# One channel tile of a 31-tap convolution: products on ScalarE, added up by accumulating DMAs

## The chip, the cores and the metric

The kernel runs on one core of one Trainium2 chip. The metric is the device time of one execution in microseconds (us), lower is better. The engines are named as in the profile: PE is TensorE (matrix products; PEld is its weight load), DVE is VectorE, ACT is ScalarE, POOL is GpSimd, SP is SyncE. An engine works through its own instruction list in order; engines wait for one another through semaphores.

## The reference

The reference runs two transformer blocks of two layers each on 512 tokens of width 1024. The change is in the second block, first layer, where the 512 tokens and 256 context tokens (768 in all) go through `conv_mixers`:

```python
def conv_mixers(h, w_in, conv_a, conv_b, conv_b_bias, ln_g, ln_b, w_out):
    p = h @ w_in
    g_b, g_c, u_a, v_b, gate_b = jnp.split(
        p, [A_WIDTH, 2 * A_WIDTH, 3 * A_WIDTH, 3 * A_WIDTH + B_WIDTH], axis=-1)
    y_a = g_b * dwconv(g_c * u_a, conv_a)
    u = v_b * jax.nn.sigmoid(gate_b)
    u = dwconv(u, conv_b) + conv_b_bias
    y_b = jax.nn.silu(layernorm(u, ln_g, ln_b))
    return jnp.concatenate([y_a, y_b], axis=-1) @ w_out
```

`conv_b` is a depthwise convolution with 31 taps over the tokens: each of its 512 channels is a sum of 31 shifted copies of its own row, each times one weight. The 512 channels are four tiles of 128. Everything is float32.

## The kernel before

Channels lie on the 128 partitions and tokens along the free dimension. A matrix product runs in "blocks": a block is one tile of 128 output channels for all tokens. Its 128x1024 weights come from HBM into `w_raw` (SP, L468), are rounded into `w_hi` by ScalarE (L675) and the remainder is written to `w_lo` by VectorE (L1201, function `split`); then TensorE multiplies high by high, high by low, and low by high (L1851, L1852, L1853). Weights have four slots and sums have four places in PSUM, so an engine can be some three blocks ahead of another. `w_hi` of a block is written three blocks ahead of its use.

The input product of the mixer has 20 blocks, in three stages:

- `mix_c`, 8 blocks: `v_b` and `gate_b`, tile by tile. After the second block of tile q, ScalarE takes the sigmoid (L791) and VectorE writes the product into the padded row `padded(q)` (L1393): `u_pad[:, q, :]` for tiles 0 to 2, `wk[:, 1, :]` for tile 3 (`wk` is a view of `work`).
- `mix_a`, 8 blocks: `g_c` and `u_a`. ScalarE copies one (L775), VectorE multiplies (L1409) and does the three-tap convolution into `conv_a` (L1411, L1335, L1338).
- `mix_b`, 4 blocks: `g_b`. VectorE multiplies by `conv_a` (L1422), ScalarE writes the high part `a_hi` (L782), VectorE the low part `a_lo` (L1313).

Then come `layernorm` and the output product `w_out`. Of `w_out` TensorE does the half that needs only `y_a` (k 0 to 3 of its first two blocks) at the head of its `layernorm`; then it waits until all four tiles of `conv_out` are there (semaphore `conv`), and sums them over the channels (L1885). The centring (L1432), squares (L800), their sums (L1890), the root on GpSimd (L523), its spreading (L1860) and the scaling (L1443) follow one after another, and the rest of `w_out` after them.

The 31-tap convolution is done wholly by VectorE, in `conv_taps(first, last)`. It numbers 124 taps (4 tiles x 31), keeps the running sum of a tile in `wk[:, 3, :]` over 783 columns (512 tokens, 15 of padding, 256 context tokens), and writes the last tap into `conv_out` (L1376, two instructions). Tap 0 of a tile is L1370, taps 1 to 29 are L1372. The taps are dealt out by hand over the blocks: 7 after each block of `mix_c` but the first, 6 after each of `mix_a`, 7 after each of `mix_b`. Each stands in VectorE's list behind the `split` of a coming block and the evacuation of the present one, so the taps fix how late VectorE comes to both. GpSimd has nothing to do from the norm's root before `mix_c` to the root of the layernorm.

Of the kernel before, what the change touches and what calls it, by code (L numbers as in the profile page):

```python
# [7 lines left out]
F32 = mybir.dt.float32  # L8
# [3 lines left out]
ALU = mybir.AluOpType  # L12
# [3 lines left out]
P = 128  # L16
D = 1024
KT_D = D // P
SEQ = 512
# [8 lines left out]
HALO = 15  # L28
U_COLS = HALO + SEQ + HALO + CTX + HALO


# [135 lines left out]
def program(nc, dram, out):  # L167
    stages = make_plan()
    stack = ExitStack()
    with stack:  # L170
# [3 lines left out]
        def sem(name):  # L174
            return stack.enter_context(nc.semaphore(name))
# [40 lines left out]
        def layout(*items):  # L216
# [9 lines left out]


        _, conv_a, u_pad, _, conv_out = layout(
            ("mix_gap", [P, 12 * D], F32), ("conv_a", [P, 4, ALL], F32), ("u_pad", [P, 3, 832], F32),
            ("mix_gap2", [P, 6 * D - 3 * 832], F32), ("conv_out", [P, 4, ALL], F32))  # L230

# [34 lines left out]
        def ps_of(st, s, a=0, b=ALL):  # L266

            if st["toks"] == SEQ:
# [29 lines left out]
        s_val = sem("gate_times_value")  # L298
        s_out = sem("out_stored")
        s_const = sem("constants_ready")  # L300
        s_constb = sem("bf16_ready")
# [17 lines left out]
        s_swt = {t: {k: sem(f"sw{t}_{k}") for k in sw_names if t == "a" or k not in only_a}  # L319
                 for t in ("a", "b")}  # L320

        LOADS_IN = 4
# [195 lines left out]
        def _(pool):  # L518
# [61 lines left out]
            for st in stages:  # L580
                if st["kind"] == "norm":
                    root(0, st["toks"] // P, s_ms, st["rms0"] + 1, s_pw)
                elif st["kind"] == "layernorm":
                    root(0, 6, s_ln["ms"], 1, s_ln["pw"])
# [35 lines left out]
        def _(act):  # L620
# [127 lines left out]
            def evac_cffn(st):  # L748
# [19 lines left out]
                return f  # L768

            def evac_mix_a(st):  # L770
                def f(b, s, i):
                    if s % 2 == 0:
                        act.wait_ge(s_mm, b + (st["block0"] + 1))
                        act.wait_ge(s_ev, b + (st["lin0"] + 4))
                        act.activation(wk[:, 0, 0:ALL], ps_lin(s), ACT.Copy).then_inc(s_gate, 1)  # L775
                        act.drain()
                return f

# [7 lines left out]
            def evac_mix_c(st):  # L786
                def f(b, s, i):
                    if s % 2 == 1:
                        act.wait_ge(s_mm, b + (st["block0"] + 1))
                        act.wait_ge(s_ev, b + (st["lin0"] + 3))  # L790
                        act.activation(wk[:, 0, 0:ALL], ps_lin(s), ACT.Sigmoid).then_inc(s_gate, 1)  # L791
                        act.drain()
                return f

# [298 lines left out]
        def _(dve):  # L1093
# [267 lines left out]
            def conv_taps(first, last):  # L1361

                n = SEQ + HALO + CTX
                acc = wk[:, 3, 0:n]
                for tap in range(first, last):
                    q, j = tap // 31, tap % 31
                    u = padded(q)
                    w = vcol("conv_b", tap)
                    if j == 0:
# [11 lines left out]
            def evac_mix_c(st):  # L1381
# [4 lines left out]
                def f(b, s, i):  # L1386
# [9 lines left out]
                    if b:  # L1396
                        conv_taps(7 * (b - 1), 7 * b)
                return f

            def evac_mix_a(st):  # L1400
                base = VEC["conv_a"][0]

                def f(b, s, i):
                    if s % 2 == 1:
# [9 lines left out]
                                   vec[:, bass.ds(q + (base + 8), 1)], ALL)  # L1414
                    conv_taps(49 + 6 * b, 55 + 6 * b)
                return f

            def evac_mix_b(st):
                def f(b, s, i):
                    t = wk[:, 2 * (s % 2), 0:ALL]  # L1420
                    dve.wait_ge(s_mm, b + (st["block0"] + 1))
                    dve.tensor_tensor(t, ps_lin(s), conv_a[:, b, :], ALU.mult).then_inc(s_ev, 1)  # L1422
                    dve.drain()
                    low_part(b, t, ALL, b + (st["tile0"] + 1))
                    dve.drain()
                    conv_taps(97 + 7 * b, min(104 + 7 * b, 124))
                return f
# [956 lines left out]
```

## Time and profile before

| | us |
|---|---|
| median of 3 runs | 3028.74 |
| lowest, highest | 3027.15, 3029.84 |
| the profiled execution | 3028.09 |
| its span, first to last instruction | 3026.3 |
| TensorE busy | 2786.0 (92%) |
| VectorE busy | 1836.8 (61%) |
| ScalarE busy | 1080.0 (36%) |
| GpSimd busy | 118.8 (4%) |

The shares are means over a program of many stages. The stretch in question lasts from about 1404.9 us (TensorE's first matmul of `mix_c`) to about 1655 us of the span; its rows stand further down. The clock column of a row, PEclk, is the share of TensorE's full clock of 2.4 GHz that was granted; 0.50 is 1.2 GHz. "us" on a row of a timeline is the time from the start of the first to the end of the last of the instructions it merges.

### The profile page before, as it was taken

What the parts mean: (1) busy time and instruction counts of PE and PEld (TensorE: products, weight loads), DVE (VectorE), ACT (ScalarE), POOL (GpSimd) and SP (SyncE); (2) the same over time, 40 slices, a digit from 0 to 9 for tenths busy, and PEclk for the clock granted to TensorE, in tenths of its full rate; (3) what the DMA queues carried; (4) which work ended last, traced back from release to release, by engine and by line L of the source; (5) the groups of instructions that cost most, each with busy time, mean ns of one, the idle gap of its engine ahead of it and who ended that gap; (6) DMA issues with size and microseconds to landing.
All of it is one profiled execution on the core that took longest, in us unless ns stands there. A gap on an engine that the chain in (4) does not pass through costs nothing.

```text
span 3026.3 us, 41051 instructions
## 1 busy us (share of the span) xinstructions
PE 2786.0 (92%) x14220; PEld 2339.0 (77%) x14220; DVE 1836.8 (61%) x2910; ACT 1080.0 (36%) x1778; POOL 118.8 (4%) x148
## 2 busy tenths in 40 slices
PE   7999899997787999998986899999997899899998
PEld 6777788886676788887875788888886787688886
DVE  6766567676565577667996554353455455564645
ACT  5444332223565322223112232232223566352432
POOL 4111000000110000000000000000000000000000
PEclk8999999998898999998997999999998999999999
DMA  3111254452001355542110122122111000232321
GB/s 110 63 56 43 98 187 167 171 182 72 29 29 36 112 180 174 175 155 68 56 49 30 48 70 70 56 65 68 54 58 42 15 29 8 70 97 91 97 89 65
DMA packets 69314, 252.07 MB, mean 83 GB/s; under 512 B 7840, under 2 KB 10144, under 8 KB 66592
## 3 DMA queue, kind: packets, MB, share of 16 engines
q1 hardware_dynamic: 69152, 249.99, 24.5%
q8 instruction: 92, 1.51, 0.2%
q14 instruction: 70, 0.57, 0.1%
HBM read 247.87 MB, written 2.10 MB: 83 GB/s over the span
## 4 chain that ended last, share of the span: by engine, by line
PE 61%; DVE 16%; issue 15%; ACT 4%; DVEq 2%; POOLq 0%; ACTq 0%; POOL 0%; DMA 0%; SPq 0%
PE psum L1852 16%; PE psum L1851 16%; PE psum L1853 16%; DVE work L1372 4%; PE psum L2233 2%; DVE w_lo L1201 1%; ACT work L991 1%; PE psum L1991 1%; ACT sw_pt L1003 1%; PE psum L1969 1%; PE psum L1971 1%; PE psum L1970 1%; DVE neg_max L1740 1%; DVE tok_ms L1489 1%; DVE w_lo L1566 1%
## 5 line engine op out<-in xcount | busy, mean ns | idle before, releaser
L1851 PE MATMUL psum<-hx_hi,w_hi 128*128 128x512 f32 x1568 | 623.9, 398 | 28.9 <-DVE w_lo L1201 13.5
L1852 PE MATMUL psum<-hx_lo,w_hi 128*128 128x512 f32 x1568 | 625.1, 399 | 0.0
L1853 PE MATMUL psum<-hx_hi,w_lo 128*128 128x512 f32 x1568 | 623.7, 398 | 0.0
L675 ACT ACTIVATE w_hi<-w_raw 128x1024 fp32r<-128x1024 f32 (+1 forms) x328 | 344.6, 1051 | 527.2 <-PE psum L1853 231.4
L1201 DVE TENSOR_TENSOR w_lo<-w_raw,w_hi 128x1024 fp32r<-128x1024 f32 (+1 forms) x328 | 397.7, 1212 | 192.6 <-ACT w_hi L675 174.0
L1851 PEld LDWEIGHTS psum<-hx_hi,w_hi 128*128 128x128 f32 x1568 | 297.1, 189 | 79.1 <-issue 16.7
L1853 PEld LDWEIGHTS psum<-hx_hi,w_lo 128*128 128x128 f32 x1568 | 297.1, 189 | 69.9
L1852 PEld LDWEIGHTS psum<-hx_lo,w_hi 128*128 128x128 f32 x1568 | 298.0, 190 | 48.4
L1851 PE MATMUL psum<-a_hi,w_hi 128*128 128x512 f32 (+1 forms) x656 | 234.1, 357 | 18.1 <-DVE a_lo L1313 10.0
L1852 PE MATMUL psum<-a_lo,w_hi 128*128 128x512 f32 (+1 forms) x656 | 234.8, 358 | 0.0
L1853 PE MATMUL psum<-a_hi,w_lo 128*128 128x512 f32 (+1 forms) x656 | 233.9, 357 | 0.0
L1851 PE MATMUL psum<-o_hi,w_hi 128*128 128x512 f32 x544 | 217.8, 400 | 5.6 <-DVE o_lo L1778 3.9
L1852 PE MATMUL psum<-o_lo,w_hi 128*128 128x512 f32 x544 | 216.8, 398 | 0.0
L1853 PE MATMUL psum<-o_hi,w_lo 128*128 128x512 f32 x544 | 216.7, 398 | 0.0
L1335 DVE SCALAR_TENSOR_TENSOR work<-psum,vec,work 128x511 f32<-128x511 f32 (+1 forms) x132 | 83.2, 658 | 164.3 <-ACT work L758 156.3
L523 POOL TENSOR_TENSOR tok_r<-tok_ms,half 128x4 f32<-128x4 f32 (+1 forms) x70 | 71.8, 1025 | 2502.2 <-DVE tok_ms L1115 1949.6
L1277 DVE SCALAR_TENSOR_TENSOR X<-psum,mods,X 128x512 f32<-128x512 f32 x96 | 60.6, 658 | 178.6 <-PE psum L1853 177.1
L1851 PEld LDWEIGHTS psum<-a_hi,w_hi 128*128 128x128 f32 x656 | 125.2, 191 | 38.5 <-DVE a_lo L1313 10.5
L758 ACT ACTIVATE work<-psum,vec 128x768 f32<-128x768 f32 (+1 forms) x88 | 70.0, 795 | 223.5 <-PE psum L1853 215.8
L1852 PE MATMUL psum<-hc_lo,w_hi 128*128 128x256 f32 x512 | 144.8, 283 | 0.0
L1851 PE MATMUL psum<-hc_hi,w_hi 128*128 128x256 f32 x512 | 144.8, 283 | 0.0
L1853 PE MATMUL psum<-hc_hi,w_lo 128*128 128x256 f32 x512 | 144.5, 282 | 0.0
(289 smaller groups left out, 4914.2 us busy)
## 6 DMA issues: line engine op xcount, KB each, us to landing
mod_w<-in_w_mod SPq DMA_DIRECT2D x96, 512.0 KB, 3.6
w_raw<-in_fup SPq DMA_DIRECT2D x88, 512.0 KB, 4.5
w_raw<-in_cup SPq DMA_DIRECT2D x88, 512.0 KB, 3.5
w_raw<-in_fdown SPq DMA_DIRECT2D x32, 512.0 KB, 4.6
w_raw<-in_cdown SPq DMA_DIRECT2D x32, 512.0 KB, 3.5
w_raw<-in_da_qkv SPq DMA_DIRECT2D x6, 1536.0 KB, 6.5
w_raw<-in_fdown SPq DMA_DIRECT2D x16, 384.0 KB, 3.1
w_raw<-in_cdown SPq DMA_DIRECT2D x16, 384.0 KB, 3.0
```

Of the source, the lines that this page charges most:

```text
L523: pool.tensor_tensor(tok_r[:, a:b], tok_ms[:, a:b], half[:, a:b], ALU.pow).then_inc(done, 1)
L675: r = act.activation(w_hi[:, off:off + n], w_raw[:, raw:raw + n], ACT.Copy)
L758: act.activation(wk[:, s, 0:toks], ps_of(st, s, 0, toks), ACT.Copy, scale=vec[:, bass.ds(b + col, 1)]).then_inc(s_ctap, 1)
L991: r = act.activation(work[:, e:e + (w1 - w0)], psum[:, w0:w1], ACT.Exp, bias=neg_max[:, col:col + 1], scale=root, accum_out=row_sum[:, col ...
L1201: r = dve.tensor_tensor(w_lo[:, off:off + n], w_raw[:, raw:raw + n], w_hi[:, off:off + n].bitcast(F32), ALU.subtract)
L1277: r = dve.scalar_tensor_tensor(X[:, b, a:e], ps_of(st, s, a, e), mods[:, l, c, bass.ds(b + o, 1)], X[:, b, a:e], ALU.mult, ALU.add)
L1335: dve.scalar_tensor_tensor(dst[:, a + 1:e], src(a, e - 1), prev, dst[:, a + 1:e], ALU.mult, ALU.add)
L1372: dve.scalar_tensor_tensor(acc, u[:, j:j + n], w, acc, ALU.mult, ALU.add)
L1851: pe.matmul(dst, wh, xh, start=first, stop=False)
L1852: pe.matmul(dst, wh, xl, start=False, stop=False)
L1853: return pe.matmul(dst, wl, xh, start=False, stop=last)
L2233: r = pe.matmul(pb[:, 5, 0:256], v_cols(tiles[k], g, p % 2), sw_pt[:, n % 2, 256 * i:256 * i + 256], start=p % 2 == 0 and k == 0, stop=p % ...
```

## The change

Tile 1 of the convolution is taken from VectorE. The running sums of that tile are two, in the two halves of `sw_vb`, a buffer that attention uses in other stages.

- **ScalarE** forms the 31 products: `tap_products` writes weight times shifted row, 783 columns, one instruction a tap (L800 and L803 of the new kernel). Taps 0 and 1 go straight into the two sums, with the bias in tap 0; taps 2 to 30 go into four buffers `tap_prod` in turn. Three products stand at the end of each block's work on ScalarE, from the fifth block of `mix_c` (after a wait for tile 1 of `u_pad`) to the sixth of `mix_a`, and the last one at its seventh. From tap 6 on each waits until the DMA that read its buffer last, that of tap j-4, has landed.
- **GpSimd** issues 29 DMAs, `tap_prod` into `sw_vb` with addition, even taps into sum 0, odd taps into sum 1. A DMA waits for its product and for the DMA before it on the same sum.
- **VectorE** keeps tiles 0, 2 and 3: 93 taps, dealt out 6 a block in `mix_c`, 4 and 5 in turn in `mix_a`, 4 a block in `mix_b` (3 in the last). In the first block of `mix_b`, behind the multiplication of the evacuation and before `low_part`, it waits for both sums and adds them into `conv_out[:, 1]`.

```diff
+                elif st["kind"] == "mix_a":
+                    for j in range(2, TAPS):
+                        pool.wait_ge(s_tapp, j + 1)
+                        if j >= 4:
+                            pool.wait_ge(s_taps[j % 2], taps_added(j - 2))
+                        pool.dma_start(tap_sum(j % 2), tap_prod[:, j % TAP_BUFS, 0:TAP_COLS], accum_op=ALU.add)\
+                            .then_inc(s_taps[j % 2], 16)
...
+            def tap_products(first, last):
+
+                u = padded(SUM_TILE)
+                for j in range(first, min(last, TAPS)):
+                    w = vcol("conv_b", TAPS * SUM_TILE + j)
+                    if j >= 2 + TAP_BUFS:
+                        act.wait_ge(s_taps[j % 2], taps_added(j - TAP_BUFS))
+                    dst = tap_sum(j) if j < 2 else tap_prod[:, j % TAP_BUFS, 0:TAP_COLS]
+                    if j == 0:
+                        act.activation(dst, u[:, j:j + TAP_COLS], ACT.Identity, scale=w, bias=vcol("conv_b_bias", SUM_TILE))\
+                           .then_inc(s_tapp, 1)
+                    else:
+                        act.activation(dst, u[:, j:j + TAP_COLS], ACT.Copy, scale=w).then_inc(s_tapp, 1)
+                    act.drain()
+
             def evac_mix_a(st):
...
+                    tap_products(12 + 3 * b, 15 + 3 * b)
...
+                    if b == 2 * SUM_TILE + 2:
+                        act.wait_ge(s_ev, st["lin0"] + 2 * SUM_TILE + 6)
+                    if b >= 2 * SUM_TILE + 2:
+                        first = 3 * (b - 2 * SUM_TILE - 2)
+                        tap_products(first, first + 3)
...
-                        conv_taps(7 * (b - 1), 7 * b)
+                        conv_taps(6 * (b - 1), 6 * b)
...
-                    conv_taps(49 + 6 * b, 55 + 6 * b)
+                    conv_taps(42 + 9 * b // 2, 42 + 9 * (b + 1) // 2)
...
+                    if b == 0:
+                        for c in range(2):
+                            dve.wait_ge(s_taps[c], taps_added(TAPS - 1 - c))
+                        for a, e, c in segs(ALL):
+                            o = HALO * c
+                            r = dve.tensor_tensor(conv_out[:, SUM_TILE, a:e], tap_sum(0)[:, o + a:o + e],
+                                                  tap_sum(1)[:, o + a:o + e], ALU.add)
+                        r.then_inc(s_ln["conv"], 1)
+                        dve.drain()
                     low_part(b, t, ALL, b + (st["tile0"] + 1))
                     dve.drain()
-                    conv_taps(97 + 7 * b, min(104 + 7 * b, 124))
+                    conv_taps(78 + 4 * b, min(82 + 4 * b, 93))
```

ScalarE's list where the sixth and seventh blocks of `mix_c` are evacuated, before: the weights of a coming block, the sigmoid of the present one, the weights of the next two.

```order
780 L675 ACTIVATE w_hi<-w_raw 128x1024 [waits block_multiplied,raw_loaded3]
781 L675 ACTIVATE w_hi<-w_raw 128x1024 [waits block_multiplied,raw_loaded0]
782 L791 ACTIVATE work<-psum 128x768 [waits psum_evacuated,block_multiplied]
783 L675 ACTIVATE w_hi<-w_raw 128x1024 [waits block_multiplied,raw_loaded1]
784 L675 ACTIVATE w_hi<-w_raw 128x1024 [waits block_multiplied,raw_loaded2]
```

The same place after the change (L696 is what L675 was, L828 what L791 was):

```order
784 L696 ACTIVATE w_hi<-w_raw 128x1024 [waits block_multiplied,raw_loaded0]
785 L828 ACTIVATE work<-psum 128x768 [waits psum_evacuated,block_multiplied]
786 L803 ACTIVATE tap_prod<-u_pad,vec 128x783 x3
787 L696 ACTIVATE w_hi<-w_raw 128x1024 [waits block_multiplied,raw_loaded1]
788 L803 ACTIVATE tap_prod<-u_pad,vec 128x783 [waits tap_added_to_sum0]
789 L803 ACTIVATE tap_prod<-u_pad,vec 128x783 [waits tap_added_to_sum1]
790 L803 ACTIVATE tap_prod<-u_pad,vec 128x783 [waits tap_added_to_sum0]
791 L696 ACTIVATE w_hi<-w_raw 128x1024 [waits block_multiplied,raw_loaded2]
```

The weights of every coming block now stand behind products, and those behind waits for the DMAs of four taps before.

VectorE's list at the last block of `mix_a` and the first of `mix_b`, before: six taps, the split, the end of tile 2 and the start of tile 3 are near; at the first block of `mix_b` only the multiplication and the low part stand ahead of the taps.

```order
1384 L1372 SCALAR_TENSOR_TENSOR work<-u_pad,vec,work 128x783
1385 L1376 SCALAR_TENSOR_TENSOR conv_out<-u_pad,vec,work 128x512
1386 L1376 SCALAR_TENSOR_TENSOR conv_out<-u_pad,vec,work 128x256
1387 L1370 TENSOR_SCALAR work<-work,vec 128x783
1388 L1372 SCALAR_TENSOR_TENSOR work<-work,vec 128x783 x3
1389 L1201 TENSOR_TENSOR w_lo<-w_raw,w_hi 128x1024 [waits w_hi_ready]
1390 L1422 TENSOR_TENSOR work<-psum,conv_a 128x768 [waits block_multiplied]
1391 L1313 TENSOR_TENSOR a_lo<-work,a_hi 128x768 [waits a_hi_ready]
1392 L1372 SCALAR_TENSOR_TENSOR work<-work,vec 128x783 x7
```

The same place after (L1243 is the split, L1465 the multiplication, L1355 the low part, L1415 a tap):

```order
1384 L1415 SCALAR_TENSOR_TENSOR work<-work,vec 128x783 x5
1385 L1243 TENSOR_TENSOR w_lo<-w_raw,w_hi 128x1024 [waits w_hi_ready]
1386 L1465 TENSOR_TENSOR work<-psum,conv_a 128x768 [waits block_multiplied]
1387 L1472 TENSOR_TENSOR conv_out<-sw_vb 128x512 [waits tap_added_to_sum1,tap_added_to_sum0]
1388 L1472 TENSOR_TENSOR conv_out<-sw_vb 128x256
1389 L1355 TENSOR_TENSOR a_lo<-work,a_hi 128x768 [waits a_hi_ready]
1390 L1415 SCALAR_TENSOR_TENSOR work<-work,vec 128x783 x4
```

The joining of the two sums has come between the multiplication and the low part, and fewer taps follow.

## Rows read from the trace of the kernel before

**Rows 1.** The chain that ended last, 1400 to 1680 us: shares by line.

```profile
by line: DVE work L1372 42.8%; DVE w_lo L1201 8.8%; issue 4.1%; PE psum L1851 3.9%; PE psum L1852 3.7%; PE psum L1853 3.7%; PE psum L1890 3.2%; PE psum L1885 2.5%; DVE hx_lo L1470 2.1%; DVE work L1479 2.1%; DVEq L1379 1.9%; DVE a_lo L1313 1
```

**Rows 2.** Waits, 1425.3 to 1622 us: who waited for whom, us, times, longest.

```profile
ACT work L775 <- DVE work L1409: 39.2, 3, 16.8
PE psum L1851 <- DVE w_lo L1201: 21.7, 4, 11.7
PE psum L1851 <- DVE a_lo L1313: 6.0, 1, 6.0
DVE a_lo L1313 <- ACT a_hi L782: 3.6, 4, 0.9
```

**Rows 3.** Timeline of VectorE: start, us, instructions merged.

```profile
1429.90 6.58 DVE L1372 SCALAR_TENSOR_TENSOR work<-u_pad,vec,work 128x783 f32<-128x783 f32 x6
1436.55 1.23 DVE L1201 TENSOR_TENSOR w_lo<-w_raw,w_hi 128x1024 fp32r<-128x1024 f32 x1
...
1469.68 1.15 DVE L1376 SCALAR_TENSOR_TENSOR conv_out<-u_pad,vec,work 128x512 f32<-128x512 f32 x2
1470.92 0.69 DVE L1370 TENSOR_SCALAR work<-u_pad,vec 128x783 f32<-128x783 f32 x1
1471.69 3.25 DVE L1372 SCALAR_TENSOR_TENSOR work<-u_pad,vec,work 128x783 f32<-128x783 f32 x3
...
1554.83 1.23 DVE L1201 TENSOR_TENSOR w_lo<-w_raw,w_hi 128x1024 fp32r<-128x1024 f32 x1
...
1564.21 0.96 DVE L1409 TENSOR_TENSOR work<-psum,work 128x768 f32<-128x768 f32 x1 [0.19 <-issue]
...
1612.32 0.96 DVE L1422 TENSOR_TENSOR work<-psum,conv_a 128x768 f32<-128x768 f32 x1
...
1620.83 1.15 DVE L1376 SCALAR_TENSOR_TENSOR conv_out<-work,vec 128x512 f32<-128x512 f32 x2
```

**Rows 4.** Timeline of VectorE: the product of `mix_c`, a 512- and a 256-column tensor_tensor.

```profile
1447.01 1.02 DVE L1393 TENSOR_TENSOR u_pad<-psum,work 128x512 f32<-128x512 f32 x2 [0.16 <-issue]
```

**Rows 5.** Timeline of ScalarE; in brackets the idle time before and its releaser.

```profile
1433.11 1.06 ACT L675 ACTIVATE w_hi<-w_raw 128x1024 fp32r<-128x1024 f32 x1 [4.97 <-PE psum L1853]
1441.45 0.82 ACT L791 ACTIVATE work<-psum 128x768 f32<-128x768 f32 x1 [7.28 <-PE psum L1853]
...
1458.25 0.81 ACT L791 ACTIVATE work<-psum 128x768 f32<-128x768 f32 x1 [7.28 <-PE psum L1853]
...
1475.05 0.81 ACT L791 ACTIVATE work<-psum 128x768 f32<-128x768 f32 x1 [7.28 <-PE psum L1853]
...
1647.66 0.93 ACT L804 ACTIVATE work<-work,vec 128x768 f32<-128x768 f32 x1
1648.67 0.84 ACT L807 ACTIVATE a_hi<-work 128x768 fp32r<-128x768 f32 x1
```

**Rows 6.** Busy time by stretch: us, PE, PEld, DVE, ACT, POOL, PEclk, DMA share, GB/s.

```profile
1424.60:1542.20 117.60, 115.77 (x661) 100.86 (x660) 108.97 (x115) 20.90 (x22) 0.00 (x0) 1.00 0.19 59
1592.30:1600.40 8.10, 0.01 (x1) 0.04 (x1) 7.56 (x8) 0.00 (x0) 0.00 (x0) 0.68 0.00 0
1622.00:1629.20 7.20, 7.12 (x16) 3.53 (x16) 0.01 (x1) 0.00 (x0) 0.00 (x0) 0.76 0.00 0
1629.20:1658.00 28.80, 21.27 (x101) 19.60 (x102) 13.80 (x15) 12.84 (x14) 1.32 (x1) 0.64 0.01 1
```

**Rows 7.** DMA issues of the whole program: KB each, median us from issue to landing.

```profile
w_raw<-in_cdown SPq DMA_DIRECT2D x16, 384.0 KB, 3.0
...
w_raw<-in_in_a SPq DMA_DIRECT2D x8, 512.0 KB, 3.5
...
w_raw<-in_g_q SPq DMA_DIRECT2D x4, 1024.0 KB, 4.9
...
second_raw<-in_da_qkv SPq DMA_DIRECT2D x2, 768.0 KB, 9.2
```

**Rows 8.** Groups of GpSimd over the whole program: count, busy us, mean ns, idle before.

```profile
L523 POOL TENSOR_TENSOR tok_r<-tok_ms,half 128x4 f32<-128x4 f32 x66 | 66.5, 1007 | 1233.7 <-DVE tok_ms L1115 923.4 <-DVE tok_ms L1491 310.3
```

More of the change, by code:

```diff
@@ L29 @@
 U_COLS = HALO + SEQ + HALO + CTX + HALO
+TAPS = 31
+TAP_COLS = SEQ + HALO + CTX
+SUM_TILE = 1
+TAP_BUFS = 4
 VEC_COLS = [("attn_norm0", 8), ("attn_norm1", 8), ("ffn_norm0", 8), ("ffn_norm1", 8), ("kv_norm", 8),
@@ L225, in program @@
             ("a_hi", [P, 8, ALL], F32R), ("a_lo", [P, 8, ALL], F32R))
-        _, conv_a, u_pad, _, conv_out = layout(
+        _, conv_a, u_pad, tap_prod, conv_out = layout(
             ("mix_gap", [P, 12 * D], F32), ("conv_a", [P, 4, ALL], F32), ("u_pad", [P, 3, 832], F32),
-            ("mix_gap2", [P, 6 * D - 3 * 832], F32), ("conv_out", [P, 4, ALL], F32))
+            ("tap_prod", [P, TAP_BUFS, 912], F32), ("conv_out", [P, 4, ALL], F32))
         _, mod_c, mod_w3, mod_out, _, mod_w = layout(
@@ L299, in program @@
         s_out = sem("out_stored")
+        s_tapp = sem("tap_product_ready")
+        s_taps = [sem(f"tap_added_to_sum{c}") for c in range(2)]
         s_const = sem("constants_ready")
@@ L320, in program, with tap_sum, taps_added @@
                  for t in ("a", "b")}
+        def tap_sum(c):
+            return sw_vb[:, c, 0:TAP_COLS]
+        def taps_added(j):
+            return 16 * (j // 2)
         LOADS_IN = 4
@@ L1361, in conv_taps @@
             def conv_taps(first, last):
-                n = SEQ + HALO + CTX
+                n = TAP_COLS
                 acc = wk[:, 3, 0:n]
+                tiles = [q for q in range(4) if q != SUM_TILE]
                 for tap in range(first, last):
-                    q, j = tap // 31, tap % 31
+                    q, j = tiles[tap // TAPS], tap % TAPS
                     u = padded(q)
-                    w = vcol("conv_b", tap)
+                    w = vcol("conv_b", TAPS * q + j)
                     if j == 0:
```

## The prediction

> **What bounds the kernel now.** TensorE is 92% busy over the program, so the first question is whether VectorE's time is worth anything in this stretch. The chain that ended last answers it: from 1400 to 1680 us it runs over the taps (L1372, 42.8%) and the splits (L1201), TensorE's blocks having under 4% a line [rows 1]. The waits say the same: TensorE stood 21.7 us for `w_lo` and 6.0 us for `a_lo`, both VectorE's, and ScalarE 39.2 us for one VectorE line; VectorE waited for others only 3.6 us, 0.9 in each block of `mix_b` for ScalarE's `a_hi` [rows 2]. The timeline of VectorE then gives places and prices [rows 3], that of ScalarE the ends of TensorE's blocks: it is released at 1433.11, 1441.45, 1458.25 and 1475.05, which is 8.4 us a block at full clock [rows 5, 6]. VectorE ends its taps at 1621.98, and TensorE starts the layernorm's sums 0.05 us later. I number the 20 blocks from 0.
>
> **What leaves VectorE.** Six plain taps take 1429.90 to 1436.55, 1.108 each; a first tap 0.77 (1470.92 to 1471.69), a last tap with its two halves 1.24 (1469.68 to 1470.92) [rows 3]. Tile 1 is 29 x 1.108 + 0.77 + 1.24 = 34.1 us.
>
> **What it gets.** The joining is two tensor_tensors of 512 and 256 columns. The nearest pair is L1393, 1.02, with 0.16 of issue ahead and 0.08 behind: 1.26 [rows 4]. It stands where VectorE idles 0.9 for `a_hi` [rows 2], so it adds 0.3. Net: -33.8 us, if every VectorE instruction can start when the one before it ends, and the sums are there.
>
> **Is TensorE the next bound?** The taps are dealt out anew, so I subtract at each place what stands ahead of it less. Block 15: before at 1564.21 [rows 3] behind 91 taps, now 73: 18 plain ones less, 1544.3. TensorE ends block 7 at 1475.05 and block 15 at 1475.05 + 8 x 8.4 = 1542.2 [rows 5]. VectorE is later by 2.1, and by 2 in all of `mix_a` (it takes 16.8 us for two blocks, as TensorE does). Block 19: before at 1612.32, less 26 plain taps, a first and a last, plus 0.3: 1581.8, against 1575.9 for TensorE. The half of `w_out` behind it ends 2.9 + 2.1 us after 1581.8, at 1586.8; the taps end at 1621.98 - 33.8 = 1588.2. So VectorE stays the bound, with TensorE 2 us behind it: this saving cannot be much enlarged, but it is not cut either.
>
> **ScalarE.** A product of 783 columns is not in the trace; 768 columns take 0.84 and 0.93, 1.01 from start to start with the drain [rows 5]. With 0.98 it is 31 x 0.98 = 30 us, 2.9 in a block. ScalarE idles 7.3 ahead of each sigmoid [rows 5], and `w_hi` is made three blocks ahead, so by itself this costs nothing. Without that cover it would be 2.9 us a block.
>
> **The adding DMAs.** Here the prediction is decided, and no row shows one. Call L the time from one DMA of a sum to the next of the same sum. From the table of issues: 512 KB land in 3.5 us, 1024 KB in 4.9 [rows 7], which is 2.1 + 1.4 per 512 KB. One tap is 128 x 783 x 4 bytes, 391 KB. An addition must read product and sum, so I count 783 KB: 4.2. GpSimd has to issue it; its small instructions take 1.0 [rows 8]. The other sum's DMA and the weights share the engines: 0.3. I take L = 5.5. Ends: 3.0 (384 KB, a plain load) and 9.2 (768 KB beside many others) [rows 7]; the first is a copy without addition, the last was in a queue at the program's start, so I stay by the sum between.
>
> What L costs: product 3 is written after the sigmoid of block 5 (1458.25 + 0.81), at 1460.1, and DMA 3 is issued then. DMA 25 is the twelfth of its sum, 3, 5 to 25, and lands at 1460.2 + 12 L at the earliest once the chain is saturated. Product 29 waits for it, and behind product 29 in ScalarE's list is `w_hi` of block 17, together 2.2 us. VectorE comes to the split of block 17 at 1554.83 [rows 3] less 16 taps, 1537.1. So nothing is lost up to 12 L = 74.7, **L = 6.2**; beyond that each us of L delays the end by 12 us, and the gain is gone at L = 6.2 + 33.8 / 12 = 9.0. With L = 5.5 the last DMA lands before 1545 while VectorE comes to the joining at about 1557, so the joining waits for nothing. Below 6.2, L doesn't matter.
>
> **The clock behind it.** The layernorm's first sums take 7.1 us at a mean granted clock of 0.76; they follow a stretch in which TensorE stood 8.1 us in one piece, its clock falling to 0.68 and less [rows 6]. Now TensorE works without a gap of over 2 us from block 0 on, as it did from 1424.6 to 1542.2 at 1.00. Those sums at full clock are 7.2 x 0.76 = 5.5: -1.7. At worst the clock is at its half there, 11 us, +3.8; at best the following stretch at 0.64 gets some too, some 4 us more [rows 6]. I take -1.7.
>
> **Sum.** The profiled execution took 3028.1, 0.6 under the median of 3028.7. 3028.1 - 33.8 - 1.7 = 2992.6, a gain of 1.2%.
>
> **Rivals.**
>
> *GpSimd is held up by VectorE.* In this kernel GpSimd has worked only in pauses of VectorE's dependents, so no row shows it issuing into a VectorE that is 93% busy (108.97 of 117.6 us, rows 6). If a DMA has to let two VectorE instructions of about 1.03 pass, L is about 7.5, the end comes 12 x 1.3 = 15.6 later, TensorE's pauses come back and with them the low clock: 3028.1 - 33.8 + 15.6 = 3010. For it: the splits and taps leave only 0.08 between them. Against: an instruction list of one engine that must wait for another's has no row here at all. The Trainium skill (SBUF — State Buffer, section "Who interferes with whom") says that VectorE instructions with two SBUF inputs contend with GpSimd's reads, and only its two-port modes lock out descriptor writing; by that rule the taps would not hold the DMAs and this rival would fall. No run here shows it yet.
>
> *The two sums' DMAs do not overlap* (the slower side). They go over one queue and the same 16 engines. If the second starts only when the first has landed, L is twice one DMA, 2 x 5.2 = 10.4: 12 x 4.2 = 50 us, against 33.8 gained, 3044. It decides from 4.5 us a DMA. The same comes out if the addition itself runs at half the rate of a load. For it: nothing here shows two DMAs of one queue at work on the same tile. Against: the 16 engines are busy to 0.19 in this stretch [rows 6], so there is room, and each sum has its own semaphore.
>
> *L near 9*, the far row: 3028.1 - 33.8 + 12 x 2.8 = 3028, no change.
>
> *VectorE's taps get longer beside the DMAs.* 93 taps at +0.1 would be 9 us; no row for or against. I count it to the first rival.
>
> **How the numbers follow.** The forecast (L up to 6.2) gets 0.60: the sum of rows is 5.5 with 0.7 to spare. GpSimd held up 0.14, L near 9 0.07, not overlapping 0.19. The likeliest case alone spans 2988 (clock) to 2998. The range takes in the first rival and L up to 9.5, 3028.1 - 33.8 + 39.6 = 3034: 2988 to 3034, leaving out the slower rival's 0.19. A measurement of this kernel can tell some 0.2%, 6 us. Faster by more: 0.60 + 0.14 = 0.74. Within: 0.07. Slower: 0.19.
>
> **What would show it.** Taps ending near 1588 instead of 1622, 93 of them at 1.03; no wait of VectorE for a sum in the first block of `mix_b`; no wait of TensorE for `w_lo` over 2 us before block 20; a clock of 1.00 up to the layernorm's sums, and these in 5.5 us. Starts of adding DMAs on one sum under 6.2 apart. Wrong would be: ScalarE idle before products with the DMA as releaser, VectorE idle before the split with `w_hi` as releaser, or taps longer than 1.03.

## The result, and the profile after

| | before | after |
|---|---|---|
| median of 4 runs, us | 3029.09 | 3000.85 |
| lowest to highest | 3027.15 to 3029.84 | 2996.45 to 3004.93 |
| the profiled execution | 3028.09 | 2996.45 |
| its span | 3026.3 | 2994.6 |

The ratio of the times is 0.9907, 95% interval 0.9892 to 0.9922: faster by 0.9%. The forecast was 2992.6 in a range of 2988 to 3034, and its direction and range held; the gain is 28.2 us by the medians and 31.6 by the profiled executions, where 35.5 were forecast. The runs of after lie further apart than those of before; eight further runs of the same kernel (below) lie between 2994.8 and 2999.7, and the median of all twelve is 2997.4.

To compare two executions I measure from the start of VectorE's `tok_ms` in the norm ahead of `mix_c` (1396.5 in before's span) and not from the start of the span, because the code ahead of it, the same in both, took 1395.7 to 1401.7 us in the profiles of this study. "Stretch" below is the time from there to the end of the last tap: 225.46 us before (to 1621.98), 195.59 after (1396.76 to 1592.35). So the spans' difference of 31.7 splits like this: -29.9 to the end of the taps, -1.7 in the layernorm's first sums, -0.7 from the centring to the scaling, +0.3 in the 1382 us behind and +0.2 ahead.

The waits of after, 1425.3 to 1592.4 us (who waited for whom, us, times, longest):

```profile
POOL sw_vb L602 <- DMA sw_vb<-tap_prod: 50.7, 23, 4.2
ACT tap_prod L803 <- DMA sw_vb<-tap_prod: 24.6, 16, 3.6
PE psum L1903 <- DVE a_lo L1355: 4.9, 1, 4.9
DVE w_lo L1243 <- ACT w_hi L696: 3.6, 1, 3.6
DVE a_lo L1355 <- ACT a_hi L819: 2.7, 3, 0.9
PE psum L1903 <- DVE w_lo L1243: 1.2, 1, 1.2
```

Of the 27.7 us that TensorE stood for VectorE [rows 2] 6.1 are left. ScalarE waits 16 times for a DMA, and a wait for ScalarE is new on VectorE: 3.6 us, once. The chain that ended last, 1400 to 1650 us of after, by line, and two of its pieces in order of time:

```profile
by line: DVE work L1415 17.4%; PE psum L1903 16.6%; PE psum L1904 16.4%; PE psum L1905 16.2%; DVE w_lo L1243 5.4%; PE psum L1942 3.3%; issue 2.2%; PE psum L1937 2.1%; DVE a_lo L1355 1.9%; PE psum L1912 1.8%; DVE work L1465 1.5%; DVE work L1
...
1495.05 1.07 ACT w_hi L696
1496.15 1.23 DVE w_lo L1243
```

In [rows 1] VectorE's taps held 42.8% and TensorE's blocks under 4% a line. Now TensorE's three lines hold 49%: the chain runs over TensorE up to 1491, crosses ScalarE's `w_hi`, and only from 1496 to 1588.8 over VectorE. Its last piece before the layernorm's sums is TensorE again, with the half of `w_out` that needs only `y_a`. VectorE's timeline (start, us, what; in brackets the idle time before and its releaser):

```profile
1488.15 4.37 DVE L1415 SCALAR_TENSOR_TENSOR work<-u_pad,vec,work 128x783 f32<-128x783 f32 x4
1496.15 1.23 DVE L1243 TENSOR_TENSOR w_lo<-w_raw,w_hi 128x1024 fp32r<-128x1024 f32 x1 [3.62 <-ACT w_hi L696]
...
1540.89 1.23 DVE L1243 TENSOR_TENSOR w_lo<-w_raw,w_hi 128x1024 fp32r<-128x1024 f32 x1
...
1548.05 0.96 DVE L1452 TENSOR_TENSOR work<-psum,work 128x768 f32<-128x768 f32 x1 [0.19 <-issue]
...
1557.03 1.03 DVE L1415 SCALAR_TENSOR_TENSOR work<-work,vec 128x783 f32<-128x783 f32 x1 [0.43 <-issue]
...
1560.58 1.03 DVE L1472 TENSOR_TENSOR conv_out<-sw_vb 128x512 f32<-128x512 f32 x2 [0.16 <-issue]
...
1591.20 1.15 DVE L1419 SCALAR_TENSOR_TENSOR conv_out<-work,vec 128x512 f32<-128x512 f32 x2
1597.86 4.11 DVE L1484 SCALAR_TENSOR_TENSOR conv_out<-psum,conv_out 128x768 f32<-128x768 f32 x4 [5.52 <-PE psum L1937]
```

The joining (L1472) has only 0.16 of issue ahead of it. The split of block 12 is the one that waits. ScalarE at that place, and at the last waits for the DMAs:

```profile
1479.41 1.06 ACT L696 ACTIVATE w_hi<-w_raw 128x1024 fp32r<-128x1024 f32 x1
1491.00 0.81 ACT L811 ACTIVATE work<-psum 128x768 f32<-128x768 f32 x1 [10.53 <-PE psum L1905]
1491.90 3.02 ACT L803 ACTIVATE tap_prod<-u_pad,vec 128x783 f32<-128x783 f32 x3
1495.05 1.06 ACT L696 ACTIVATE w_hi<-w_raw 128x1024 fp32r<-128x1024 f32 x1
...
1537.20 0.95 ACT L803 ACTIVATE tap_prod<-u_pad,vec 128x783 f32<-128x783 f32 x1 [3.59 <-DMA sw_vb<-tap_prod]
1538.29 1.06 ACT L696 ACTIVATE w_hi<-w_raw 128x1024 fp32r<-128x1024 f32 x1
```

ScalarE stood 10.5 us for the first block of `mix_a`, then wrote three products and only then the weights. GpSimd's issues of adding DMAs 12 and 13, and of the last two:

```profile
1493.15 0.87 POOL L602 DMA_DIRECT2D sw_vb<-tap_prod  x1 [6.88 <-ACT tap_prod L803]
1494.26 0.89 POOL L602 DMA_DIRECT2D sw_vb<-tap_prod  x1 [0.24 <-issue]
...
1542.45 0.88 POOL L602 DMA_DIRECT2D sw_vb<-tap_prod  x1 [1.93 <-DMA sw_vb<-tap_prod]
1544.77 0.87 POOL L602 DMA_DIRECT2D sw_vb<-tap_prod  x1 [1.43 <-DMA sw_vb<-tap_prod]
```

Sum 0 has nine steps in (1544.77 - 1493.15), 5.74 each; sum 1 has eight in (1542.45 - 1494.26), 6.02 each. Last, the row of the DMAs (KB each, median us to landing) and stretches in the columns of [rows 6]:

```profile
sw_vb<-tap_prod POOLq DMA_DIRECT2D x29, 391.5 KB, 5.5
```

```profile
1424.60:1542.20 117.60, 117.60 (x674) 102.65 (x673) 105.36 (x113) 52.30 (x55) 23.91 (x27) 1.00 0.70 153
1450.00:1545.00 95.00, 95.00 (x544) 82.78 (x543) 84.63 (x92) 44.31 (x46) 24.55 (x29) 1.00 0.83 174
1592.50:1597.90 5.40, 5.33 (x17) 2.85 (x16) 0.04 (x1) 0.00 (x0) 0.00 (x0) 1.00 0.00 0
```

In the same stretch TensorE is busy 117.6 us (115.77 in [rows 6]), and the DMA engines 0.70 of it instead of 0.19.

The last row above holds the layernorm's first sums, at a clock of 1.00. Just ahead of them the clock was low. TensorE stood 4.95 us for the last `a_lo`, up to 1588.89, and then did the half of `w_out`, in this stretch (same columns):

```profile
1588.80:1592.40 3.60, 3.51 (x12) 3.00 (x13) 3.25 (x5) 0.00 (x0) 0.00 (x0) 0.57 0.02 7
```

The clock is 0.50 from 1590.80 to 1591.80 and 0.91 in the half us behind that, so it came back to full some 0.6 us before the sums began at 1592.45. This half of `w_out` ends with the taps (1592.35), and TensorE no longer stands for them, as it did for 2.7 us in before.

### The profile page after: what moved, and what is told of

It is laid out like the page before. It is cut to its first block, busy times and chain, and to the rows that moved or that the text cites. A ratio compares the mean times of both kernels' runs of the same rounds, so it can differ in the third digit from the quotient of the medians.

```text
span 2994.6 us, 41110 instructions
## 1 busy us (share of the span) xinstructions
PE 2778.4 (93%) x14220; PEld 2331.4 (78%) x14220; DVE 1806.4 (60%) x2880; ACT 1110.6 (37%) x1809; POOL 145.1 (5%) x177
## 3 DMA queue, kind: packets, MB, share of 16 engines
q0 software_dynamic: 4176, 11.63, 2.2%
## 4 chain that ended last, share of the span: by engine, by line
PE 65%; issue 15%; DVE 12%; ACT 4%; DVEq 2%; POOLq 1%; ACTq 0%; POOL 0%; DMA 0%; SPq 0%
PE psum L1904 17%; PE psum L1903 17%; PE psum L1905 17%; PE psum L2285 2%; DVE work L1415 1%; ACT work L1033 1%; PE psum L2043 1%; DVE w_lo L1243 1%; ACT sw_pt L1045 1%; PE psum L2021 1%; PE psum L2022 1%; PE psum L2023 1%; DVE neg_max L1792 1%; PE psum L2274 1%; DVE tok_ms L1541 1%
## 5 line engine op out<-in xcount | busy, mean ns | idle before, releaser
L696 ACT ACTIVATE w_hi<-w_raw 128x1024 fp32r<-128x1024 f32 (+1 forms) x328 | 344.8, 1051 | 512.3 <-PE psum L1905 207.2
L1243 DVE TENSOR_TENSOR w_lo<-w_raw,w_hi 128x1024 fp32r<-128x1024 f32 (+1 forms) x328 | 397.7, 1213 | 195.3 <-ACT w_hi L696 176.4
## 6 DMA issues: line engine op xcount, KB each, us to landing
sw_vb<-tap_prod POOLq DMA_DIRECT2D x29, 391.5 KB, 5.5
```

The source lines that it names most:

```text
L696: r = act.activation(w_hi[:, off:off + n], w_raw[:, raw:raw + n], ACT.Copy)
L1243: r = dve.tensor_tensor(w_lo[:, off:off + n], w_raw[:, raw:raw + n], w_hi[:, off:off + n].bitcast(F32), ALU.subtract)
```

## The experiments

After the first reading the theory was: the adding DMAs cost nothing, since they are just fast enough; the 4 us that are missing come from where three products stand on ScalarE. The rival was that the DMAs cost them, and widen the spread.

**The changed kernel once more,** with nothing edited.

> The changed kernel unchanged, for a second profile beside the first (2996.5 us, spread of its four runs 2996 to 3005). Theory A (additions on the edge): each adding DMA takes 5.5 us from issue to landing with the 16 DMA engines over 90% busy; ScalarE's list then reaches the weights of block 17 within 1.5 us of VectorE's need, so executions in which the DMAs run a little slower lose some us there. Expect 2996 to 3006, and in a slower profile VectorE idle before splits with ScalarE's w_hi as releaser, ScalarE idle before products with the DMA as releaser. Theory B (the spread comes from elsewhere): the same waits as in the first profile, 3.6 us in all, and the time lost outside 1425 to 1600 us.

Measured: 2998.1 (2995.93 to 2999.65), ratio 0.9897 (0.988 to 0.9913). Stretch 195.72, with the same wait of 3.6 us for `w_hi`, as theory B had it. What is explained is therefore not one odd execution.

**The products without the DMAs.**

```diff
-                    for j in range(2, TAPS):
-                        ...
+                    pass
...
-                    if j >= 2 + TAP_BUFS:
-                        act.wait_ge(s_taps[j % 2], taps_added(j - TAP_BUFS))
...
-                        for c in range(2):
-                            dve.wait_ge(s_taps[c], taps_added(TAPS - 1 - c))
+                        dve.wait_ge(s_tapp, TAPS)
```

> GpSimd issues no adding DMA and ScalarE does not wait for any; products and the joining stay, so tile 1 has only its first two taps. Theory A: the 3.6 us at block 12 stay (they come from three products of 1.0 us behind the copy of block 8), all else is gone: 2996 with a spread under 2 us, 4 to 5 us under the changed kernel's median. If the 3.6 us are the DMAs' doing: 2992. If DMAs slow VectorE or TensorE down in themselves: more than 6 us under.

Measured: 2997.42 (2993.95 to 2999.45), ratio 0.9898 (0.9882 to 0.9915), stretch 195.58. The wait stays, in the view of waits over 1425 to 1605 us:

```profile
DVE w_lo L1236 <- ACT w_hi L691: 3.6, 1, 3.6
```

So 29 adding DMAs, which keep 16 engines busy to 0.83, cost the stretch of this kernel nothing. Theory A was right on the wait and wrong on the spread, expected under 2 us: it is 5.5 without the DMAs, and 2.8, 3.7 and 8.5 in the three sets of runs with them.

**Products 12 to 14 ahead of the copy of block 8,** instead of behind it.

```diff
                 def f(b, s, i):
+                    if b == 0:
+                        tap_products(12, 15)
                     if s % 2 == 0:
...
-                    tap_products(12 + 3 * b, 15 + 3 * b)
+                    if b > 0:
+                        tap_products(12 + 3 * b, 15 + 3 * b)
```

> Products 12 to 14 stand ahead of the copy of block 8 instead of behind it. Blocks 8 and 9 end together at about 1491 (TensorE does the first two blocks of a stage in turns), so in the changed kernel products 12 to 14 and behind them the weights of block 12 start only then, and VectorE idles 3.6 us. Theory A: here that wait falls to under 1 us, the adding DMAs get the 7 us in which GpSimd idled there, and the spread falls: 2991 to 2995. Theory B (the wait is the DMAs' doing): the 3.6 us only move elsewhere, 2996 to 3004.

Measured: 2992.22 (2990.97 to 2994.44), ratio 0.9877 (0.9861 to 0.9894). The wait for `w_hi` falls from 3.6 to 0.5, but the stretch only from 195.7 to 194.36, because another wait takes its place (waits of this kernel, 1425 to 1605 us, whose lines are shifted by 3):

```profile
DVE work L1468 <- PE psum L1908: 1.9, 1, 1.9
...
DVE w_lo L1246 <- ACT w_hi L696: 0.5, 1, 0.5
```

VectorE waits for TensorE's first block of `mix_b`. Both waits have one cause, in the function by which TensorE begins every product:

```python
            def pair(st, k0, k1):
                ...
                for k in range(k0, k1):
                    operand(st, k)
                    step(st, 0, k)
                    step(st, 1, k)
```

Blocks 0 and 1 of a stage are done step by step in turn, so the first ends only one step before the second, and not 8.4 us before it: block 8 at 1491, not 1483.4; block 16 at about 1558, not 1550.6. This is read from the order of the code and from the times at which the waiting engines are released; no run undid the order. It stood in the trace of before too, where ScalarE was released for the copy of block 8 a full 17.4 us after block 7:

```profile
1492.48 0.81 ACT L775 ACTIVATE work<-psum 128x768 f32<-128x768 f32 x1 [15.42 <-PE psum L1853]
```

At the centring of the kernel with the products moved only 0.7 of the 1.3 us is left (it starts 200.40 us from `tok_ms`, in the changed kernel 201.10): TensorE does the half of `w_out` at 0.50 to its end here, ends it 0.5 us after the taps, and starts the sums only then.

**Tile 1 left out altogether:** no products, no DMAs, and in place of the joining one memset, so the output lacks that tile.

```diff
-                    tap_products(12 + 3 * b, 15 + 3 * b)
...
-                        tap_products(first, first + 3)
...
-                        for a, e, c in segs(ALL):
-                            ...
+                        dve.memset(conv_out[:, SUM_TILE, :], 0.0).then_inc(s_ln["conv"], 1)
```

> Tile 1 is left out altogether: no products on ScalarE, no adding DMAs, no joining (a row of zeros takes its place), VectorE keeps its 93 taps dealt out as in the changed kernel. It prices all that the change adds. Theory C: the wait at block 12 falls from 3.6 to about 0.5 us and a wait of about 2 us for TensorE's block 16 comes in its place: 193.5 to 194.5 us from the norm's TOK_MS to the last tap, only 1 to 2 us under the changed kernel's 195.7. The prediction's picture (TensorE 2 us ahead of VectorE everywhere): 191.5.

Measured: 2994.65 (2992.19 to 2996.61), ratio 0.989 (0.9874 to 0.9907), stretch 194.14, with the same 1.9 us for TensorE, as theory C had it. This is the floor of the stretch for this order of VectorE's list: all that the change adds on ScalarE, GpSimd and the DMA queue costs 195.6 - 194.1 = 1.5 us, and with three products moved 0.2. At the centring (200.29) it is 0.8 and 0.1.

**One adding DMA in flight:** each also waits for the one before it, on the other sum.

```diff
+                        if j >= 3:
+                            pool.wait_ge(s_taps[(j - 1) % 2], taps_added(j - 1))
```

> Each adding DMA waits for the one before it on the other sum too, so only one is in flight. Theory A (12 us for each us of the time L between DMAs of one sum beyond 6.2): one DMA alone takes about 4.5 us from issue to landing, L is 9.0 to 9.4, the end comes 34 to 38 us later than without a delay: 3026 to 3034, about the time of the kernel before. If the two sums' DMAs do not overlap in the changed kernel anyway: no difference to it, 3001. If the additions are hidden: also 3001.

Measured: 3032.16 (3023.84 to 3039.77), ratio 1.0009 (0.9997 to 1.0022), stretch 228.38. Its waits over 1425 to 1605 us, two issues of GpSimd six apart, and the row of the DMAs:

```profile
ACT tap_prod L805 <- DMA sw_vb<-tap_prod: 64.5, 22, 4.4
...
DVE w_lo L1245 <- ACT w_hi L698: 33.3, 6, 8.6
...
DVE conv_out L1474 <- DMA sw_vb<-tap_prod: 3.1, 1, 3.1
```

```profile
1488.26 0.86 POOL L604 DMA_DIRECT2D sw_vb<-tap_prod  x1 [4.43 <-DMA sw_vb<-tap_prod]
...
1515.82 0.88 POOL L604 DMA_DIRECT2D sw_vb<-tap_prod  x1 [3.69 <-DMA sw_vb<-tap_prod]
```

```profile
sw_vb<-tap_prod POOLq DMA_DIRECT2D x29, 391.5 KB, 4.0
```

Starts are (1515.82 - 1488.26) / 6 = 4.6 apart, so one sum gets a DMA every 9.2 us. By the prediction's working that is 12 x (9.2 - 6.2) = 36 us beyond the 225.5 - 33.8 = 191.7 of a stretch that nothing delays: 227.7, against 228.4. The total agrees better than its parts. The split of block 17 comes 32.9 us later than in the changed kernel without its 3.6 (36 by the working), and the joining waits 3.1 us for the last DMA, which the working did not have. The whole gain is gone. The chain of DMA, product, `w_hi`, split is thereby shown, and with it what the second sum is for: the overlap of two DMAs is worth 33 us.

**Three products' room instead of four,** to see how near the changed kernel is to that (the layout keeps the fourth buffer's place).

```diff
-TAP_BUFS = 4
+TAP_BUFS = 3
...
-                        act.wait_ge(s_taps[j % 2], taps_added(j - TAP_BUFS))
+                        act.wait_ge(s_taps[(j - TAP_BUFS) % 2], taps_added(j - TAP_BUFS))
```

> Only edit: product j waits for adding DMA j-3 instead of j-4. Theory A (an adding DMA takes 5.5 us with two in flight, starts on one sum some 5.9 us apart, and four products' worth of room just hides that): product 29 now waits for DMA 26, landing near 1539.5, so w_hi of block 17 ends near 1541.7 where VectorE needs it at 1540.9. VectorE waits 1 to 2 us more, and from the start of norm's first instruction to the end of the last tap it takes 196.5 to 198.0 us (195.6 to 195.7 in the changed kernel). Theory B (there is more slack than that, ScalarE being ahead): 195.5 to 195.9, no further wait. A single look's total is about 3000 to 3003 by A, uncertain by 3 us through the stretch before.

Measured: stretch 198.42, 2.8 longer and 0.4 over the expected range. The mechanism was right, the place not: the wait comes three blocks sooner, at block 14. ScalarE and VectorE of this kernel there:

```profile
1514.78 0.95 ACT L803 ACTIVATE tap_prod<-u_pad,vec 128x783 f32<-128x783 f32 x1 [2.96 <-DMA sw_vb<-tap_prod]
1515.87 1.06 ACT L696 ACTIVATE w_hi<-w_raw 128x1024 fp32r<-128x1024 f32 x1
```

```profile
1516.96 1.23 DVE L1243 TENSOR_TENSOR w_lo<-w_raw,w_hi 128x1024 fp32r<-128x1024 f32 x1 [2.80 <-ACT w_hi L696]
```

Yet its one time was 2995.94, no worse than the changed kernel's. From the start of the centring it took 1392.2 us where three profiles of the changed kernel took 1396.7 to 1396.9. About half of the difference goes with TensorE's clock in the first 85 us of it; 1.9 us lie behind the next norm and were not followed. The windows 10 to 15 us after the layernorm's `tok_ms`, in before, after, the kernel with products moved (second time) and this one, in that order:

```profile
1650.08:1655.08 5.00, 5.00 (x23) 4.39 (x22) 3.65 (x5) 4.25 (x5) 0.00 (x0) 0.69 0.00 0
```

```profile
1618.05:1623.05 5.00, 5.00 (x18) 4.32 (x17) 3.65 (x5) 4.28 (x5) 0.00 (x0) 0.54 0.00 0
```

```profile
1618.58:1623.58 5.00, 5.00 (x24) 4.37 (x23) 3.66 (x5) 4.29 (x5) 0.00 (x0) 0.74 0.00 0
```

```profile
1621.66:1626.66 5.00, 5.00 (x25) 4.36 (x24) 3.65 (x5) 4.29 (x5) 0.00 (x0) 0.79 0.00 0
```

TensorE is busy in all four, but after the change its clock comes back last. It also falls first: the next norm's `tok_ms`, in before and in after, waits longer for TensorE's sums.

```profile
1714.38 0.17 DVE L1115 TENSOR_SCALAR tok_ms<-psum 128x6 f32<-128x6 f32 x1 [1.59 <-PE psum L1872]
```

```profile
1684.26 0.17 DVE L1157 TENSOR_SCALAR tok_ms<-psum 128x6 f32<-128x6 f32 x1 [2.81 <-PE psum L1924]
```

The mean clock of the 5 us that begin 70 us after the layernorm's `tok_ms` is 0.95 in before and 0.76 in after. From that `tok_ms` to the next norm's it takes 76.2 us after the change, in the other three 74.0 to 74.3. So the changed kernel loses 1.9 us there against before, in each of its three profiles, some 0.7 ahead of that last wait and 1.2 in it. Behind that norm it is 1.6 us shorter than before, which I did not follow; what sets the moments at which the clock returns and falls I did not test either.

**Are the moved products worth having?** The kernel with products 12 to 14 moved and the changed one, again, both on the same chip, as the first time.

> Products 12 to 14 ahead of block 8's gate copy, once more on the same chip as the changed kernel. Theory A (the 3.6 us wait for w_hi(12) is the order on ScalarE, and 1.3 us of it is real gain): stretch 194.2 to 194.5 us against 195.6 to 195.7, median 1 to 4 us under the changed kernel's. Theory B (the earlier 6 us between the two medians was the drift of the stretch before): stretch as by A, but medians within 1 us of each other.

> The changed kernel with nothing edited, beside early_2. Both theories: stretch 195.6 to 195.8 us, ratio to the kernel before 0.988 to 0.991, and w_hi of block 12 waited for by VectorE for 3.6 us. A: 1 to 4 us slower than early_2; B: within 1 us of it.

Measured: moved 2996.1 (2991.5 to 2998.05), stretch 194.35; unmoved 2996.38 (2994.77 to 2997.6), stretch 195.60. The stretch repeats to 0.1 us in both, the total does not: 5.9 us apart the first time, 0.3 the second, with means over eight runs of 2994.0 and 2997.1. The 1.3 us are shown. In the profiles there is more: from `tok_ms` ahead of `mix_c` to the end of the program the two of the moved kernel take 1594.4 and 1594.5 us, the three of the changed one 1597.8 to 1598.1. Of these 3.4 us 0.7 are there at the centring, 0.7 more at the layernorm's `tok_ms`, and 2.1 go with the clock in the 76 us behind it, not with a wait that the order on ScalarE took away. What else differs between these profiles lies ahead of `tok_ms`. The medians were expected within 1 us of each other by theory B, and the second time they were; by the times alone the moved kernel is not shown to beat the changed one.

**Two taps moved as well,** from `mix_b` to the last block of `mix_a`, where VectorE waited 1.9 us for TensorE.

```diff
-                    conv_taps(42 + 9 * b // 2, 42 + 9 * (b + 1) // 2)
+                    conv_taps(42 + 9 * b // 2, 80 if b == 7 else 42 + 9 * (b + 1) // 2)
...
-                    conv_taps(78 + 4 * b, min(82 + 4 * b, 93))
+                    conv_taps(80 + 4 * b, min(84 + 4 * b, 93))
```

> The order of the run 'early', and two taps of VectorE moved from mix_b into the last block of mix_a, where VectorE stood 1.9 us for TensorE's block 16. Theory C (TensorE's interleaved pair of blocks 16 and 17 is the next bound: both end together near 1558): these two taps (2.2 us) fill the wait, VectorE comes to block 16 with TensorE, and the taps end 1.9 us sooner than in 'early'. From the norm's TOK_MS instruction to the end of the last tap: 192.5 us, against 194.4 in 'early' and 195.7 in the changed kernel; median some 2 us under 'early', 2990. Theory D (the wait is TensorE being held by VectorE's own splits): TensorE moves along, the taps end 0 to 0.3 us sooner only.

Measured: 2994.1 (2992.5 to 2998.31), ratio 0.9886 (0.9869 to 0.9902). The stretch falls to 192.77, near theory C's 192.5, but the median is not the 2990 that it expected, and the centring starts at 200.83, against 200.40 with the products moved alone. TensorE's last work before the sums is late now:

```profile
PE psum L1906 <- DVE a_lo L1358: 5.0, 1, 5.0
```

```profile
1590.00:1595.00 5.00, 1.77 (x5) 1.49 (x6) 3.32 (x5) 0.84 (x1) 0.00 (x0) 0.52 0.35 105
1595.00:1600.00 5.00, 5.00 (x16) 3.21 (x16) 0.00 (x0) 0.00 (x0) 0.00 (x0) 0.79 0.00 0
```

As in the kernels above it stands 5 us for the last `a_lo`, drops to about half its clock, and does the half of `w_out` at that rate. Here that work ends 2.7 us after the taps (195.5 from `tok_ms`), where with the products moved alone it was 0.5. So the saving on VectorE ends here.

**What in a DMA takes the time.** One execution each. In one the DMAs copy instead of adding; in the other they add only the first 392 columns.

```diff
-                        pool.dma_start(tap_sum(j % 2), tap_prod[:, j % TAP_BUFS, 0:TAP_COLS], accum_op=ALU.add)\
+                        pool.dma_start(tap_sum(j % 2), tap_prod[:, j % TAP_BUFS, 0:TAP_COLS])\
```

```diff
-                        pool.dma_start(tap_sum(j % 2), tap_prod[:, j % TAP_BUFS, 0:TAP_COLS], accum_op=ALU.add)\
+                        pool.dma_start(tap_sum(j % 2)[:, 0:392], tap_prod[:, j % TAP_BUFS, 0:392], accum_op=ALU.add)\
```

> The 29 DMAs copy instead of adding, with the same waits. Theory: an addition reads its target too, a copy doesn't, so of the 5.5 us from issue to landing the copy should save the second reading: by the slope of the loads, 1.1 us alone and more beside the other sum's, 3.5 to 4 us; ScalarE's waits for DMAs fall from 24 us to a few. If the addition costs nothing in itself, 5.5 stays.

> Each DMA adds 392 columns of 783. One DMA alone took 4.0 us from issue to landing in the run 'serial'. By a fixed part of 2.1 us and a part by size, half the size gives 3.0 us, and the DMA engines' share halves; ScalarE's waits for DMAs fall under 5 us. If the cost is by descriptor (128 rows stay 128 rows), it stays at 5 or more with the engines as busy.

Measured: 3000.78 copying and 3003.92 with half the columns. Neither is faster, as for a chain that hides the DMAs: the stretches are 195.72 and 195.32, while a single time is uncertain by some us. ScalarE's waits for DMAs fall to 1.4 and 4.5 us, as expected; the copy takes less than the 3.5 to 4 us expected for it. The rows of the DMAs, issues and the queue over 1447 to 1550 us (packets, MB, share of the 16 engines' time), for copying, for adding 392 columns, and the queue for adding 783:

```profile
sw_vb<-tap_prod POOLq DMA_DIRECT2D x29, 391.5 KB, 2.9
...
q0 software_dynamic: 2320, 11.63, 29.1%
```

```profile
sw_vb<-tap_prod POOLq DMA_DIRECT2D x29, 196.0 KB, 3.2
...
q0 software_dynamic: 4176, 5.82, 34.1%
```

```profile
q0 software_dynamic: 4168, 11.61, 62.8%
```

The same bytes cost twice the engine time when they are added (62.8% against 29.1%). Half the bytes in as many packets cost half of it (34.1%), so the packets are not the price.

## Why the prediction held, point by point

- **What leaves VectorE, -34.1, and the joining, +0.3.** Right in size. The stretch fell by 29.9; with the two gaps named below, 3.6 and 0.4, that is 33.9. The 93 taps take 1.03 each as before, beside the DMAs too.
- **"So VectorE stays the bound, with TensorE 2 us behind it."** Wrong, and this is the step that failed. The prediction subtracted on VectorE's side and counted 8.4 us a block on TensorE's, but took the first block of a stage to end 8.4 after its start. It ends some 7.5 later, since the first two go in turn. In before it cost nothing, as VectorE was later than both, but it stood in the trace (17.4 us from block 7 to block 8 on ScalarE). The 33.8 was not to be had with this order: even without tile 1's work at all the stretch is 194.1, a gain of 31.3.
- **ScalarE, "by itself this costs nothing".** Wrong in one block of 20. A product takes 0.95, 1.03 from start to start (0.98 forecast). The idle time that should cover it lay there, 10.5 us ahead of the copy of block 8, but the products stood behind that copy. `w_hi` of block 12 then waited for them, and VectorE for it, 3.6 us. Moving them gave 1.3 back; of the rest 0.5 stayed and 1.9 became a wait for TensorE. ScalarE's waits for DMAs, 24.6 us in 16, were named as a sign of being wrong; with `w_hi` still in time behind all of them they cost nothing, so that sign was too strict.
- **Block 15 and the end.** The prediction had block 15's product at 1544.3 and the last tap at 1588.2; they came at 1548.05 and 1592.35, late by the 3.6 and, for the last tap, by 0.43 us of issue at 1557.03.
- **The adding DMA, L = 5.5 against a limit of 6.2.** It decided rightly, with some luck. The sum was near, its terms were not: alone, one takes 4.0 to landing and 4.6 to the next start (forecast 4.2 + 1.0), and with the other sum's DMA beside it 5.7 to 6.0, so that one adds 1.1 to 1.4 (forecast 0.3). Two misses of opposite sign made up for each other in part. `w_hi` of block 17 was ready at 1539.35, VectorE came at 1540.89: 1.5 us to spare (1.3 at block 16), not 12 x 0.7 = 8.4, although the 3.6 us of block 12 had made VectorE later. Room for three products is already too little. The last DMA was forecast to land before 1545 and was only issued at 1544.77, but VectorE came to the joining at 1560.42, so the joining waited for nothing, as forecast.
- **The price beyond the limit, 12 us for each us of L.** Shown in the main with one DMA in flight: 228.4 measured, 227.7 by that working, of which 33 lie on the path that it names and 3.1 at the joining, where it had no wait.
- **The clock, -1.7.** Right in size, by luck: from the last tap to the centring it took 5.51 us instead of 7.21, at a clock of 1.00 instead of 0.76. The reason given failed. TensorE was to work without a gap of over 2 us and at 1.00 up to these sums; it stood 4.95 us for the last `a_lo`, and its clock was 0.57 in the work that follows (1588.80 to 1592.40). It came back some 0.6 us before the sums. With the products moved TensorE stands just as long, the clock comes back 0.3 us after the sums have begun, and from the last tap to the centring it takes 6.0 us. The half of `w_out` was to end at 1586.8 and ended at 1592.5, 4.2 us of that because VectorE came to block 19 at 1586.01 instead of 1581.8, the rest by the low clock, and so it ends with the taps and not 1.4 us before them. The squares' sums gained a further 0.7. Behind them 1.9 was lost again by the clock's later return and earlier fall, which the prediction had only as a possible gain.
- **GpSimd held up by VectorE.** It fell. The instruction takes 0.87 us (0.86 to 1.10 over 29) and follows its release at once, beside a VectorE that is busy 84.6 of 95 us. By the rule cited from the Trainium skill (SBUF — State Buffer, section "Who interferes with whom") the taps should not hold it; this trace agrees.
- **The two sums' DMAs don't overlap.** Not so: up to two are in flight, though they lengthen each other. Where they are kept apart the kernel is as slow as before, at 4.6 us a DMA or 9.2 per sum, which is near the rival's threshold of 4.5; its 3044 rested on 5.2 a DMA.
- **The sum.** Of the 3.9 us by which the profiled 2996.45 missed 2992.6, the stretch makes 3.9, and 0.2 of time ahead stands against 0.4 less behind the centring. The other runs lie up to 8.5 us higher without a change in the kernel; the clock and the part ahead of the stretch move a total by some us from run to run.

## What to carry to other kernels

When work leaves the bounding engine, take the end of each block of the next engine from its own instruction order, first blocks of a stage above all, and not from a mean time a block: that is what decides how much of the saving arrives. Work that fills an engine's idle time has to stand ahead of the wait that makes the idle time, or it delays what is behind the wait. And a running sum kept by adding DMAs needs several independent sums: the latency of one DMA after another, not the bytes, was what would have cost the gain.

## What the runs showed of the hardware

- An adding DMA of 391.5 KB within SBUF takes 4.0 us to landing by itself and 5.5 with a second in flight; a copy of the same size takes 2.9, and an addition of half the size 3.2 (the last two also with up to two in flight). GpSimd's issue of it takes 0.87 and 0.88 us (medians) for the two additions and 0.55 for the copy.
- An adding DMA makes 4176 / 29 = 144 packets at either size, the copy 2320 / 29 = 80; the queue takes 62.8% of the 16 engines' time against 29.1%, and 34.1% for the addition of half the size.
- The loads of `in_in_a` feel it: a median of 4.0 us instead of 3.5 [rows 7], without anyone waiting for them.
- TensorE's clock over the same work after the same stand of 4.95 us: 0.57 in the changed kernel (1588.80 to 1592.40), 0.50 with the products moved, where it was back at 1.00 only 0.3 us into the sums.
- The same stretch repeats within 0.1 us from profile to profile (195.59, 195.72, 195.60), while whole runs of the same kernel are up to 10 us apart. A gain under some 3 us is seen in the stretch, and not surely in the total.
